# First expert group's rows by indirect DMA, the meta rows' transposes copied earlier, the sink attention's keys projected once

## What is computed

```python
def swa_sink_attention(q, k, v, sinks):      # 4 query heads, 2 key heads, window 128
    ...
    scores = jnp.einsum('bnqhgd,bnkhd->bnhgqk', qb, kk) * (d ** -0.5)
    ...
    probs = jax.nn.softmax(jnp.concatenate([scores, sink], axis=-1), axis=-1)[..., :-1]

def hier_moe(h, w_grp, b_grp, w_rtr, b_rtr, w1, w3, w2):
    grp_prob = jax.nn.softmax((t @ w_grp).astype(F32) + b_grp, axis=-1)
    g_prob, g_sel = lax.top_k(grp_prob, 1)                      # one group of 8 experts
    ...
    e_prob, e_sel = lax.top_k(jax.nn.softmax(in_grp, axis=-1), TOP_K_IN_GROUP)   # two of them
    ...
    hid = jax.nn.silu(jnp.einsum('td,edf->tef', t, w1)) * jnp.einsum('td,edf->tef', t, w3)
    y = jnp.einsum('tef,efd->td', hid * combine[..., None].astype(hid.dtype), w2)
    return y.reshape(bsz, seq, d)
```

## Time and profile before

| | us |
|---|---|
| median of three runs | 1447.62 |
| lowest, highest | 1447.08, 1450.34 |
| the profiled execution | 1452.82 |
| its span, first to last instruction | 1451.0 |
| TensorE busy with matmuls | 1361.5 (94%) |
| VectorE, ScalarE, POOL busy | 554.2, 456.2, 38.2 |
| mean granted clock of TensorE | 0.965 of 2.4 GHz |

### The profile page before, as it was taken

The page is one execution under the profiler, slowest core; times in us unless marked ns, Lnnn a source line. Parts: engine busy times, 40 slices in busy tenths (PEclk is TensorE's granted clock), DMA queues, the critical chain, the costliest instruction groups (busy, mean ns, idle before and its releaser), DMA issues.

```text
span 1451.0 us, 18735 instructions
## 1 busy us (share of the span) xinstructions
PE 1361.5 (94%) x7343; PEld 859.2 (59%) x7343; DVE 554.2 (38%) x1212; ACT 456.2 (31%) x1007; POOL 38.2 (3%) x58
## 2 busy tenths in 40 slices
PE   6999989999899999989999999799998979999997
PEld 5777567775687877555433343588776654333432
DVE  2234212351477384431212222668485331222114
ACT  3145332453463134321111121564234412112121
POOL 0000000000002000000000000002000000000000
PEclk9999999999999999978999999899999979999999
DMA  9552252331431132554999999132132557999993
GB/s 352 110 166 88 87 206 93 111 116 58 179 117 60 59 124 80 203 204 179 394 422 420 421 422 398 40 113 89 38 138 85 207 203 283 407 421 422 422 422 131
DMA packets 48668, 307.96 MB, mean 212 GB/s; under 512 B 5685, under 2 KB 6197, under 8 KB 16960
## 3 DMA queue, kind: packets, MB, share of 16 engines
q1 hardware_dynamic: 43872, 287.56, 50.3%
q0 software_dynamic: 3520, 9.95, 2.8%
q10 hardware_dynamic: 1184, 9.18, 1.7%
HBM read 300.99 MB, written 8.59 MB: 213 GB/s over the span
## 4 chain that ended last, share of the span: by engine, by line
PE 80%; DVE 13%; ACT 5%; issue 1%; DMA 0%; DVEq 0%; ACTq 0%
PE ps L1010 22%; PE ps L1638 16%; PE ps L1664 8%; PE ps L1256 4%; PE ps L1724 4%; PE ps L1044 4%; PE ps L1703 4%; PE ps L1533 1%; PE ps L1475 1%; DVE projT L2521 1%; PE ps L1218 1%; DVE small L2520 1%; PE ps L1647 1%; PE ps L1481 1%; PE ps L1465 1%
## 5 line engine op out<-in xcount | busy, mean ns | idle before, releaser
L1010 PE MATMUL ps<-hT,ring 128*128 128x272 f32 (+1 forms) x2016 | 482.6, 394 | 7.0 <-ACT projT L1845 3.1
L1010 PEld LDWEIGHTS ps<-hT,ring 128*128 128x128 f32 x2016 | 381.9, 193 | 85.1 <-issue 10.7
L1638 PE MATMUL ps<-ring,arena 128*64 128x512 f32 x384 | 168.8, 604 | 0.0
L1638 PE MATMUL ps<-projT,arena 128*64 128x512 f32 x496 | 167.2, 595 | 1.1 <-DVE arena L2843 1.1
L1664 PE MATMUL ps<-ring,arena 128*64 128x512 f32 x384 | 116.0, 596 | 0.0
L1638 PEld LDWEIGHTS ps<-projT,arena 128*64 128x64 f32 x496 | 49.0, 137 | 101.6 <-issue 101.4
L2842 DVE TENSOR_TENSOR arena<-arena,ps 128x256 f32<-128x256 f32 x32 | 13.5, 421 | 244.5 <-ACT arena L2206 244.5
L1664 PEld LDWEIGHTS ps<-ring,arena 128*64 128x64 f32 x384 | 34.5, 137 | 70.2 <-issue 70.2
L1954 ACT ACTIVATE projT<-ps 128x272 f32<-128x272 f32 x68 | 27.0, 397 | 144.9 <-PE ps L1010 143.4
L1638 PEld LDWEIGHTS ps<-ring,arena 128*64 128x64 f32 x384 | 47.0, 138 | 33.2 <-issue 33.1
L2852 DVE COPY arena<-ps 128x512 f32<-128x512 f32 x64 | 44.1, 690 | 49.9 <-PE ps L1664 49.8
(11 more groups left out here) (476 smaller groups left out, 1674.9 us busy)
## 6 DMA issues: line engine op xcount, KB each, us to landing
ring<-experts SPq DMA_DIRECT2D x96, 1024.0 KB, 11.9
ring<-w_in SPq DMA_DIRECT2D x64, 1024.0 KB, 4.9
projT<-experts SPq DMA_DIRECT2D x62, 1024.0 KB, 12.3
arena<-experts SPq DMA_DIRECT2D x18, 1024.0 KB, 12.9
ring<-w_out SPq DMA_DIRECT2D x16, 1024.0 KB, 4.8
prm<-experts SPq DMA_DIRECT2D x16, 1024.0 KB, 13.4
prm<-params ACTq DMA_DIRECT2D x2, 2048.0 KB, 7.9
prm<-params ACTq DMA_DIRECT2D x2, 1152.0 KB, 10.5
```

The costliest lines, as they stand in the source:

```text
L1010: mm = pe.matmul(ps[:, 5 + j % banks, 0:ncols], w[:, j % 2, k, :], hT[:, k, T - ncols:T], start=(k == 0), stop=(k == KC - 1))
L1638: mm = pe.matmul(ps[64 * e:64 * e + 64, 0, :], xg[:, 4 * h + k, i % 2, 64 * e:64 * e + 64], w[e][:, k // 2, 512 * (k % 2):512 * (k % 2) + ...
```

## The change

Three edits.

1. **Sink attention.** The keys are projected as one chunk: key head 0 on rows 0 to 63, key head 1 on rows 64 to 127. The query heads are laid out in the order 0, 2, 1, 3, so that a head still meets its key on the same rows. There are 28 chunks and 14 weight items per layer, and the steps of the list move one chunk up from the rotation on, which now follows `latent_v` in the same gap. `score_place` keeps the heads of the sink attention in plain order.
2. **Meta rows' transposes.** In layer 0 ScalarE copies them ahead of the squares of tile 2.
3. **First group's rows.** `gather_first` and its copies are gone. `first_tokens` multiplies `xsel` with two columns of row codes; VectorE turns the result into row numbers between the two choices of experts; POOL waits for them and for all stores of normed rows, and fetches group 0 like the others. `xrows` is cleared once per layer ahead of the routing. TensorE waits for the fetch before the first pair. The same wait takes the place of `group_rows_copied` in the branch for crowded experts, which does not run here.

```diff
-MQ, MKV, MKR, SV, DV, SQ, SK, DQ, DK, CB, CC, CX, GATE = 0, 2, 3, 4, 5, 7, 9, 11, 13, 15, 17, 19, 21
-N1 = 29
+MQ, MKV, MKR, SV, DV, SQ, SK, DQ, DK, CB, CC, CX, GATE = 0, 2, 3, 4, 5, 7, 9, 10, 12, 14, 16, 18, 20
+N1 = 28
...
-    after = {3: [("latent_sums",)], 5: [("latent_q",)], 6: [("latent_k",)], 7: [("latent_v",)], 8: [("latent_rot",)],
-             9: [("tokens",)], 10: [("scores", 0)], 11: [("scores", 1)], 12: [("turn", 0)], 13: [("weigh", 0), ("scores", 2)],
...
+    after = {3: [("latent_sums",)], 5: [("latent_q",)], 6: [("latent_k",)], 7: [("latent_v",), ("latent_rot",)],
+             8: [("tokens",)], 9: [("scores", 0)], 10: [("scores", 1)], 11: [("turn", 0)], 12: [("weigh", 0), ("scores", 2)],
...
             if job[0] == "swa":
-                return projT[r, SQ + h // 2, qc], projT[r, SK + h // 2, kcols]
+                r = slice(64 * (h // 2), 64 * (h // 2) + 64)
+                return projT[r, SQ + h % 2, qc], projT[r, SK, kcols]
...
+        def score_place(job, h):
+
+
+            return h if job[0] == "swa" else place(h)
...
-            for h in range(4):
+            for h in (0, 2, 1, 3) if job[0] == "swa" else range(4):
                 q, k = job_qk(job, h)
-                mm = pe.matmul(job_scores(job)[:, place(h), :], q, k, start=True, stop=True)
+                mm = pe.matmul(job_scores(job)[:, score_place(job, h), :], q, k, start=True, stop=True)
...
-                            pe.wait_ge(s("projection_copied"), SK + 2)
+                            pe.wait_ge(s("projection_copied"), SK + 1)
...
-                def gather_first():
+                def first_tokens():
 
 
                     pe.wait_ge(s("group_selected"), 1)
-                    for half in range(2):
-                        for t in tiles:
-                            n = ROWS[t]
-                            mm = pe.matmul(ps[:, 2 + half, :], xsel[0:n, t, :], res[0:n, t, 512 * half:512 * half + 512],
-                                           start=(t == t0), stop=(t == 2))
-                        mm.then_inc(s("group_rows_done"), 1)
+                    for t in tiles:
+                        n = ROWS[t]
+                        mm = pe.matmul(ps[:, 2, 0:2], xsel[0:n, t, :], const("row_codes")[0:n, 2 * t:2 * t + 2],
+                                       start=(t == t0), stop=(t == 2))
+                    mm.then_inc(s("group_rows_done"), 1)
...
-                gather_first()
+                first_tokens()
...
                     pe.wait_ge(s("pairs_selected"), group + 1)
-                    if i:
-                        pe.wait_ge(rows_fetched, 16 * ((GROUPS - 1) * l + group))
-                    else:
-                        pe.wait_ge(s("group_rows_copied"), 2)
+                    pe.wait_ge(rows_fetched, 16 * (GROUPS * l + group + 1))
...
+                    def turned_rows_in(q):
+
+                        u = norm_order(l)[q]
+                        for half in range(2):
+                            a.wait_ge(s("router_in_turned"), 2 * q + half + 1)
+                            L(a.activation(h2T[:, 4 * half:4 * half + 4, COL[u]:COL[u] + ROWS[u]],
+                                           ps[:, 6 + half, 0:4 * ROWS[u]].rearrange("p (k n) -> p k n", k=4), ACT.Copy),
+                              s("router_in_copied"))
+
                     for p, t in enumerate(norm_order(l)):
                         n = ROWS[t]
                         if t == 2:
                             a.wait_ge(s("out_projected"), len(tiles_of(l)) + 1)
                             a.sem_inc(ring_used, ITEMS_WO)
                             mixer_ends(a)
+                        if t == 2 and l < LAYERS - 1:
+                            turned_rows_in(1)
                         square_sums(t)
-                        if t == 0:
-                            continue
-                        for q in range(p if t == 1 else 1, p + 1):
-                            u = norm_order(l)[q]
-                            for half in range(2):
-                                a.wait_ge(s("router_in_turned"), 2 * q + half + 1)
-                                L(a.activation(h2T[:, 4 * half:4 * half + 4, COL[u]:COL[u] + ROWS[u]],
-                                               ps[:, 6 + half, 0:4 * ROWS[u]].rearrange("p (k n) -> p k n", k=4), ACT.Copy),
-                                  s("router_in_copied"))
+                        if t:
+                            turned_rows_in(p)
                     a.wait_ge(s("choices_ready"), 1)
                     t0 = tiles_of(l)[0]
                     L(a.activation(lg[:, t0:, 40:44], lg[:, t0:, 40:44], ACT.Exp))
                     L(a.activation(lg[:, t0:, 99:100], lg[:, t0:, 99:100], ACT.Exp), s("choice_exps_ready"))
-
-                    for half in range(2):
-                        a.wait_ge(s("group_rows_done"), half + 1)
-                        a.activation(xrows[:, 512 * half:512 * half + 512], ps[:, 2 + half, :], ACT.Copy)\
-                            .then_inc(s("group_rows_copied"), 1)
...
+                V(v.memset(xrows, 0.0))
                 v.wait_ge(s("logits_done"), 1)
...
                     if k == 0:
                         V(v.scalar_tensor_tensor(out=c(164, 32), in0=c(132, 32), scalar=NEG, in1=c(64, 32),
                                                  op0=ALU.mult, op1=ALU.add))
+                        v.wait_ge(s("group_rows_done"), 1)
+                        V(v.tensor_scalar(group_tokens[:, 0:1], ps[:, 2, 0:1], -1.0, float(NO_ROW), ALU.mult, ALU.add),
+                          s("group_tokens_ready"))
                 V(v.tensor_tensor(c(352, 32), c(132, 32), c(196, 32), ALU.add), s("experts_chosen"))
...
                     v.wait_ge(s("pairs_selected"), g + 1)
+                    if g == 0:
+                        return
                     VP(v.tensor_reduce(mx[:, 0:1], xplaces[:, 2 * PER_GROUP:3 * PER_GROUP], AX, ALU.add))
                     VP(v.tensor_scalar(group_tokens[:, g:g + 1], mx[:, 0:1], -0.5, float(NO_ROW - T // 2), ALU.mult, ALU.add),
                        s("group_tokens_ready"))
...
                 for group in range(GROUPS):
                     g.wait_ge(s("group_tokens_ready"), group + 1)
+                    if group == 0:
+                        g.wait_ge(rows_stored, 16 * (3 * l + len(tiles_of(l))))
+                    if GROUPS * l + group:
+                        g.wait_ge(rows_fetched, 16 * (GROUPS * l + group))
+                    g.indirect_dma_start(xrows, None, normed_rows,
+                                         bass.IndirectOffsetOnAxis(ap=group_tokens[:, group:group + 1], axis=0),
+                                         bounds_check=T - 1, oob_is_err=False).then_inc(rows_fetched, 16)
                     if group:
-                        g.wait_ge(rows_stored, 16 * (3 * l + len(tiles_of(l))))
-                        if group > 1:
-                            g.wait_ge(rows_fetched, 16 * ((GROUPS - 1) * l + group - 1))
-                        g.indirect_dma_start(xrows, None, normed_rows,
-                                             bass.IndirectOffsetOnAxis(ap=group_tokens[:, group:group + 1], axis=0),
-                                             bounds_check=T - 1, oob_is_err=False).then_inc(rows_fetched, 16)
                         send(l, group - 1)
...
-    kv0, kv1 = r[1][:64], r[1][64:]
+    queries = r[0].reshape(4, 64)[[0, 2, 1, 3]].reshape(-1)
     gates = [r[12][256 * i:256 * i + 256] for i in GROUP_ORDER]
-    cols1 = np.concatenate([r[6], r[7], np.tile(r[8], 4), r[2], r[11], r[0], kv0, kv0, kv1, kv1, r[9], r[10],
-                            r[3], r[4], r[5], *gates, np.tile(r[8], 4)])
+    cols1 = np.concatenate([r[6], r[7], np.tile(r[8], 4), r[2], r[11], queries, r[1], r[9], r[10], r[3], r[4], r[5], *gates])
...
-                           col(f["group_norm"], KC), rows(f["attn_sinks"][:, [0, 2, 1, 3]])], 2)
+                           col(f["group_norm"], KC), rows(f["attn_sinks"])], 2)
```

More of the change, by code:

```diff
@@ L88, in mixer_order_1 @@
 def mixer_order_1():
-    after = {3: [("latent_sums",)], 5: [("latent_q",)], 6: [("latent_k",)], 7: [("latent_v",)], 8: [("latent_rot",)],
-             9: [("tokens",)], 10: [("scores", 0)], 11: [("scores", 1)], 12: [("turn", 0)], 13: [("weigh", 0), ("scores", 2)],
-             14: [("turn", 1)], 15: [("weigh", 1), ("scores", 3)], 16: [("turn", 2), ("square", 0)], 17: [("weigh", 2), ("norm", 0)],
-             18: [("turn", 3)], 19: [("weigh", 3), ("square", 1)], 20: [("norm", 1), ("stick_z",)],
-             21: [("stick_soft",), ("conv", 0)], 22: [("conv", 1)], 23: [("stick_sums",)], 24: [("square", 2)],
-             25: [("stick_probs",), ("norm", 2)], 26: [("stick_out",), ("square", 3)], 27: [("norm", 3)]}
+    after = {3: [("latent_sums",)], 5: [("latent_q",)], 6: [("latent_k",)], 7: [("latent_v",), ("latent_rot",)],
+             8: [("tokens",)], 9: [("scores", 0)], 10: [("scores", 1)], 11: [("turn", 0)], 12: [("weigh", 0), ("scores", 2)],
```

(12 more changed lines are left out.)

## The result

The kernel after takes 1436.5 us (median of 8 runs, 1434.8 to 1443.2) beside 1449.8 of the kernel before (median of 8 runs, 1447.1 to 1452.5): ratio 0.9926, interval 0.9908 to 0.9943, that is **10.7 us less** (8.3 to 13.3). The plain difference of the two medians is 13.3. A second measurement gave the ratio 0.9926 again. The forecast was 1432.6, in a range of 1429.0 to 1438.0: the direction is right and the time lies in the range, but the saving by the ratio is seven tenths of the 15.0 us of the sum, and 15.0 lies outside its interval. That it landed in the wide range is in part luck.

The account below looks back on a forecast made before the run. TensorE was taken to bound the kernel (94% of the span), so only less work or waiting there saves time. 7.0 + 1.8 + 5.1 + 1.1 = 15.0 us off the 1447.6 median gave 1432.6 us, range 1429.0 to 1438.0.

Parts of the forecast that it names:

- Keys, 7.0: First mixers: one of 29 projection chunks goes in each layer, 3.5 us of TensorE each, 7.0 us less for two.
- Rival 4: First mixers: the removed chunk was cover, so VectorE's and ScalarE's attention chains take the 7 us back: 1439.6; chance 0.04.
- Meta copies, 1.8: Layer 0's router: copies fall into ScalarE's idle time, norm to routing takes 6.42 us for 8.18, 1.8 us less.
- Rival 3: Layer 0's router: the copies' new place does nothing, as ScalarE's squares would wait for the transposes: 1434.4; chance 0.05.
- rival 2: Layer 0's router: the clock stays up as TensorE's idle time is filled, 2.7 us more: 1428.8 to 1430.8; chance 0.08.
- Fetch, layer 0, 5.1: Layer 0's routing: without the gather 7.7 us go, less 0.2 for VectorE and 2.3 for counting at 1.2 GHz: 5.1.
- Fetch, layer 1, 1.1: Layer 1's routing: the first pair's gather starts at 1195.0 in place of 1196.07, 1.1 us less.
- The clock, 1.2 on either side: After the first pair's gather starts: the instant the clock rises varies between runs, 1.2 us either way.

Follow-up runs that it names:

- the second trace: The kernel before, unchanged, profiled once more: its profiled execution took 1447.4 us with a span of 1445.6.
- the first trace: The unchanged kernel before, in the profiled execution on which the forecast rests: 1452.8 us.
- after_warm: The kernel after plus 128x512 matrix products that nobody reads in TensorE's waits of both layers' router and routing: 1439.7 us, ratio 0.9943.

## Why the prediction came out as it did

- **Keys, 7.0.** Right, if a little high. 3.2 and 3.25 us at the two rotations against the second trace, 6.3 at layer 0's router; 5.8 (3.3 to 8.3) in the runs of the keys alone. Rival 4 is out.
- **Meta copies, 1.8.** Right as a distance (6.41 us for 6.42). Up to the slots it gave 1.4 against the first trace and 2.4 against the second, in which the meta rows' logits stood at 1.2 GHz. What was left out: the time that it saves is followed by 1.2 GHz products whose length isn't fixed. Alone, the 2.7 us of its trace were given back by a gather 2.8 longer. Rival 3 is out; so is rival 2 (the clock of after is 0.51 from 620 to 628).
- **Fetch, layer 0, 5.1.** This is the term that was mis-sized, and the step that failed. Against the first trace it measured 4.9, with its pieces nearly as forecast. Against the second it is 2.0 up to the gather, and 0.7 of that goes back behind it, 0.5 at the first pair, whose products run while the clock is still low: 1.3. The price was read from a trace of 1452.8 us, in which the removed products ran wholly at 1.2 GHz, and taken off the median of 1447.6: "nothing in its stretches tells why, so I take the difference to the median". A second trace tells why: of its 5.4 us less, 2.9 lie between slots and gather, where the very products that the change removes took 8.65 us for 11.49. The sum counts those 2.9 as saved. In the runs of the fetch alone both its terms together, 6.2, measured -0.1 (1.4 more to 1.3 less).
- **Fetch, layer 1, 1.1.** 1.3, and 0.9 more behind the gather.
- **The clock, 1.2 on either side.** Too small, and at the wrong place. I let it move only behind the first gather. It moves at the start (2.2), inside the removed products (2.8), and by whole stretches of 3.4 us in unchanged dense work, each worth about 1.6.

With 6.3 and 2.4 for the first two terms, 1.3 in place of 5.1 and 2.2 in place of 1.1 the sum is 6.3 + 2.4 + 1.3 + 2.2 = 12.2 us, what the traces differ by. That lies between the 10.7 of the ratio and the 13.3 of the medians, inside the interval. What is left can't be put down to a cause: both profiled executions stand under the medians of their runs, that of after by 1.3 us and the second of before by 2.4 (against 1449.8), and four of the fourteen runs of after stood at 1439.8 or above. The base of the forecast, the median of three runs, was also 2.2 us under that of eight. Which pattern of the clock an execution gets, and why fetch alone nearly always got a bad one, stays open.

## What to carry to other kernels

Where a profile's execution stands away from the median, take a second one, count matmul records per busy microsecond stretch by stretch in both, and find the difference before subtracting: a price read from instructions at 1.2 GHz needn't be that of the usual run. Dense products that an edit removes from a thin stage may be what brings the clock back, so cost what follows them at the low clock too. Here unread products fitted to TensorE's waits gave 4 to 6 us more, and only once each had been measured and none stood where the clock had already fallen.

## What the runs showed of the hardware that was not expected

- Three parts gave 5.8, 1.0 and -0.1 us apart and 10.7 together. The 4.0 between are about the uncertainty of such a sum, so that they don't add is likely and not shown; the 5.4 us between two traces of one kernel are clear.
- The same instructions at nearly the same time (1036 to 1046) ran at 0.83 of the clock in one kernel and 0.66 in another whose mixer starts alike.
- In after TensorE was recorded busy 6.19 of 7.00 us from 636 to 643 and stood at 0.50 all the same. With unread products of 128x512 in the waits of this stage and the ones before (after_warm), it ran at 1.00.
- The fetch of the first group's rows landed 3.2 to 3.4 us after its issue in layer 0, in nine traces of kernels with the fetch, and 4.1 to 6.7 in layer 1, where the stream of weights was still ending; it took 5.5 to 8.7 beside the experts' weights.
